# A streaming-encoder layer with 64 experts: expert outputs scattered with an add into two sums per token, in place of one row per token and choice

## The reference, cut to what matters

```python
def moe_ffn(h, ...):
    scores = sigmoid(t @ w_router)
    ...                                   # 4 of 8 groups, then top 8 of 64 experts: idx
    gate = sel / sum(sel) * 2.5
    yb = (silu(xb @ we_gate[e]) * (xb @ we_up[e])) @ we_down[e]     # for each block of tokens of an expert
    routed = segment_sum(yb * gate, tok)                            # 8 rows a token
    shared = (silu(t @ ws_gate) * (t @ ws_up)) @ ws_down
    return routed + shared

x = x + gt2 * rmsnorm(moe_ffn(h, ...), norm_ffn_post)
```

## Time and profile before

| what | value |
|---|---|
| median of 3 runs | 1409.8 us |
| the profiled execution | 1406.37 us |
| its span, first to last instruction | 1404.6 us |
| granted TensorE clock, mean | 0.965 of full speed |
| busy: TensorE, VectorE, ScalarE, GpSimd | 1297.7, 1010.8, 617.2, 256.0 us |
| experts, first instruction to the barrier | 618.7 to 1352.2 us |
| last stage | 1352.2 to 1404.6 us |
| moved by DMA | 340.8 MB, 243 GB/s over the span |

### The profile page before, as it was taken

How to read it: one execution, slowest core, us unless ns; L and a number is a source line. 1 busy time by engine, 2 the same in 40 slices (tenths; PEclk the granted TensorE clock), 3 DMA queues, 4 the chain that set the end, 5 groups by cost and what they waited for, 6 DMA issues and landing times. The chain is left out here.

```text
span 1404.6 us, 18781 instructions
## 1 busy us (share of the span) xinstructions
PE 1297.7 (92%) x5779; PEld 914.4 (65%) x5779; DVE 1010.8 (72%) x1651; ACT 617.2 (44%) x944; POOL 256.0 (18%) x329
## 2 busy tenths in 40 slices
PE   4999999858998999969999999999999999999947
PEld 4878888546884444536767677676776767776613
DVE  5879999789343523646878888788887888878617
ACT  3523222542242013134656566565665656656401
POOL 0000000250000000012233232332323323232200
PEclk9899999979998999989999999999999999999979
DMA  9773353100017321328999999999999999989268
GB/s 351 279 255 132 110 173 113 60 1 1 1 61 288 110 90 60 150 103 325 347 356 351 349 358 349 356 350 359 381 380 363 344 343 348 351 321 328 105 260 346
DMA packets 86890, 340.82 MB, mean 243 GB/s; under 512 B 17122, under 2 KB 22452, under 8 KB 59708
## 3 DMA queue, kind: packets, MB, share of 16 engines
q1 hardware_dynamic: 66960, 306.51, 58.3%
q0 software_dynamic: 19584, 33.60, 6.6%
q10 hardware_dynamic: 300, 0.11, 0.0%
HBM read 333.87 MB, written 44.04 MB: 269 GB/s over the span
## 5 line engine op out<-in xcount | busy, mean ns | idle before, releaser
L2261 DVE TENSOR_TENSOR gate_up_low<-gate_up,gate_up_high 128x1024 fp32r<-128x1024 f32 x204 | 244.6, 1220 | 42.5 <-ACT gate_up_high L2152 42.5
L2233 PE MATMUL py<-down_ring,hT 128*128 128x512 f32 x544 | 250.0, 602 | 1.0 <-ACT hT L2171 0.9
L2194 PE MATMUL p_gate_up<-gate_up_high,x_hi 128*128 128x512 f32 x544 | 242.4, 446 | 5.3 <-DVE x_lo L2270 5.3
L2194 PE MATMUL p_gate_up<-gate_up_low,x_hi 128*128 128x512 f32 x544 | 216.8, 398 | 0.0
L2194 PE MATMUL p_gate_up<-gate_up_high,x_lo 128*128 128x512 f32 x544 | 215.4, 396 | 0.0
L2152 ACT ACTIVATE gate_up_high<-gate_up 128x1024 fp32r<-128x1024 f32 x204 | 203.7, 1051 | 0.3 <-PEq L1415 0.3
L2233 PEld LDWEIGHTS py<-down_ring,hT 128*128 128x128 f32 x544 | 98.0, 190 | 99.0 <-issue 98.9
L2194 PEld LDWEIGHTS p_gate_up<-gate_up_high,x_hi 128*128 128x128 f32 x544 | 103.9, 191 | 44.6 <-issue 20.9
L2123 POOL TENSOR_TENSOR carrier<-offsets 1x1 f32<-1x1 f32 x136 | 30.7, 226 | 517.8 <-DVE tokens L2279 471.1
L2194 PEld LDWEIGHTS p_gate_up<-gate_up_high,x_lo 128*128 128x128 f32 x544 | 103.5, 190 | 30.1 <-issue 11.0
L2176 ACT ACTIVATE y<-py 128x512 f32<-128x512 f32 x68 | 40.7, 599 | 180.1 <-PE py L2233 180.1
(11 more groups left out here) (361 smaller groups left out, 1928.6 us busy)
## 6 DMA issues: line engine op xcount, KB each, us to landing
down_ring<-in_we_down SPq DMA_DIRECT2D x68, 1024.0 KB, 9.5
gate_up<-in_we_gate SPq DMA_DIRECT2D x51, 1024.0 KB
gate_up<-in_we_up SPq DMA_DIRECT2D x51, 1024.0 KB
x_again<-in_we_gate SPq DMA_DIRECT2D x17, 1024.0 KB
x_again<-in_we_up SPq DMA_DIRECT2D x17, 1024.0 KB
ring<-in_w_in SPq DMA_DIRECT2D x8, 2048.0 KB, 7.9
ring<-in_w_ada SPq DMA_DIRECT2D x16, 1024.0 KB, 5.9
rows<-expert_rows SPq DMA_DIRECT2D x6, 2048.0 KB, 18.5
```

The source lines that it names most:

```text
L2194: mm = pe.matmul(pgu[u % 2][:, :], x[:, u % 2, k, :], weights, start=(k == 0 and n == 0), stop=(k == KD - 1 and n == 2))
L2233: mm = pe.matmul(py[half][:, :], hT[:, u % 2, k, :], weights[:, k, half * N:half * N + N], start=(k == 0), stop=(k == 1))
L2261: V.tensor_tensor(moe.low[u % RING][:, :, piece(i), :], moe.gate_up[u % RING][:, :, piece(i), :], exact(w_hi[:, u % 2, :, piece(i), :]), A ...
```

## The change

A block's outputs are no longer scattered to rows of their own. There are two arrays in DRAM of one row a token; blocks of even number are scattered with an add to the first, those of odd number to the second. The first is preset with the shared expert's output, the second with zeros, both by SyncE at the start of `experts`; the zeros come from the two `y` buffers, which GpSimd clears first. A scatter waits for the scatter two blocks back, that is the one before it into the same array. The row number is the token number, so the rank and the third table value go. The last stage loads two rows a token, 4 MB in place of 16.8 MB, adds them on VectorE, and doesn't use TensorE.

```diff
             def tabulate():
-                for t in range(NT):
-                    link.sign(V.tensor_tensor_scan(rank[:, t, :], keep.ones[:, 0:NE], sel[:, t, :], 0.0, ALU.mult, ALU.add))
...
-                link.sign(V.tensor_tensor(rank, rank, sel, ALU.subtract))
...
-                for t in range(NT):
-                    link.sign(V.tensor_scalar(values[:, t, :, 2], rank[:, t, :], tokf[:, 2, t:t + 1], None, ALU.add))
...
-    moe.parts = m.sb("table_parts", [P, NT, NE, 3, 3], BF16)
+    moe.parts = m.sb("table_parts", [P, NT, NE, 2, 3], BF16)
...
-    moe.rows = nc.dram_tensor("expert_rows", (S * TOPK, D), F32, kind="Internal").ap()
+    moe.sums = [nc.dram_tensor(f"expert_sums{i}", (S, D), F32, kind="Internal").ap() for i in range(2)]
...
             sp.wait_ge(s_x, 1)
+            sp.dma_start(moe.sums[0].rearrange("(t p) d -> p t d", p=P), moe.shared[:, :, :]).then_inc(s_start, 16)
+            sp.wait_ge(s_zero, 1)
+            for half in range(2):
+                sp.dma_start(moe.sums[1][half * S // 2:(half + 1) * S // 2, :].rearrange("(t p) d -> p t d", p=P),
+                             y[:, :, :]).then_inc(s_blank, 16)
             for b in range(RING - 1):
                 moe.load_down(sp, b, b)
...
         def _(pool):
+            pool.memset(y[:, :, :], 0.0).then_inc(s_zero, 1)
...
                 pool.wait_ge(s_yV, b + 1)
+                if isinstance(b, int) and b < 2:
+                    pool.wait_ge(*((s_start, 16), (s_blank, 32))[b])
+                left(pool, b, u)
                 carry_wait(s_scatter, b, 1)
-                pool.indirect_dma_start(moe.rows, bass.IndirectOffsetOnAxis(row_ids[:, u % 4, 0:1], 0), y[:, u % 2, :], None,
-                                        bounds_check=last_row, oob_is_err=False).then_inc(s_out[u % 2], 16)
+                pool.indirect_dma_start(moe.sums[u % 2], bass.IndirectOffsetOnAxis(row_ids[:, u % 4, 0:1], 0), y[:, u % 2, :], None,
+                                        bounds_check=last_token, oob_is_err=False,
+                                        compute_op=ALU.add).then_inc(s_out[u % 2], 16)
...
             def y_half(b, u, first):          # on ScalarE and on VectorE
+                if isinstance(b, int) and b < 2:
+                    act.wait_ge(s_blank, 32)
...
-                    mm = pe.matmul(pid[:, 0:9], hot[:, u % 2, t, :], column[:, u % 2, t, :], start=(t == 0), stop=(t == NT - 1))
+                    mm = pe.matmul(pid[:, 0:6], hot[:, u % 2, t, :], column[:, u % 2, t, :], start=(t == 0), stop=(t == NT - 1))
...
-                V.tensor_tensor(row_ids[:, u % 4, :], number[:, u % 4, 2:3], moe.offsets[:, 1:2], ALU.add).then_inc(s_rows, 1)
+                V.tensor_tensor(row_ids[:, u % 4, :], number[:, u % 4, 1:2], moe.offsets[:, 0:1], ALU.add).then_inc(s_rows, 1)
```

The new last stage (the old one's loads, products, tree and halves go):

```diff
+            for t in range(NT):                                    # SyncE
+                for kind, tile in enumerate((y, more)):
+                    sp.dma_start(tile[:, t, :], moe.sums[kind][t * P:(t + 1) * P, :]).then_inc(s_in[t], 16)
...
+                act.activation(sq[:, :], y[:, t, :], ACT.Square, accum_out=total[:, t:t + 1]).then_inc(s_sq, 1)
+                act.wait_ge(s_sq, t + 1)
+                act.activation(mean[:, t:t + 1], total[:, t:t + 1], ACT.Copy, bias=D * RMS_EPS).then_inc(s_whole, 1)
...
+            def gated(t):                                          # VectorE
+                dve.wait_ge(s_in[t], 32)
+                V.tensor_tensor(y[:, t, :], y[:, t, :], more[:, t, :], ALU.add).then_inc(s_y, 1)
+                dve.wait_ge(s_y, t + 1)
+                V.scalar_tensor_tensor(out=scaled[:, t, :], in0=y[:, t, :], scalar=D ** 0.5, in1=keep.gate2[:, :],
+                                       op0=ALU.mult, op1=ALU.mult).then_inc(s_gt, 1)
...
+            gated(0)
+            for t in range(NT):
+                if t + 1 < NT:
+                    gated(t + 1)
+                finish(t)
```

More of the change, by code:

```diff
@@ L1407 @@
 MAXB = NE + S * TOPK // P - 1
-NO_TOKEN, NO_ROW = 8 * S, 16 * S * TOPK
+NO_TOKEN = 8 * S
 BIG = 1e30
@@ L1441, in merge_route @@
         g8 = old(NT, NG, 8)
-        scores, biased, sel, gated, left, rank = (old(NT, NE) for _ in range(6))
-        values = old(NT, NE, 3)
+        scores, biased, sel, gated, left = (old(NT, NE) for _ in range(5))
+        values = old(NT, NE, 2)
         gs, top4, top8 = (old(NT, 8) for _ in range(3))
         gleft, gmask = old(NT, NG), old(NT, NG)
-        total, over, tokf, pf, bf = old(NT), old(NT), old(3, NT), old(1), old(4)
+        total, over, tokf, pf, bf = old(NT), old(NT), old(2, NT), old(1), old(4)
         before = old(P)
@@ L1791, in _ @@
             link.sign(V.tensor_scalar(tokf[:, 1, :], tokf[:, 0, :], float(-NO_TOKEN), None, ALU.add))
-            link.sign(V.tensor_scalar(tokf[:, 2, :], tokf[:, 0, :], float(TOPK), float(-NO_ROW), ALU.mult, ALU.add))
             dve.wait_ge(s_x, 16)
@@ L1867, in tabulate @@
                     link.sign(V.tensor_scalar(values[:, t, :, 1], sel[:, t, :], 0.0, tokf[:, 1, t:t + 1], ALU.mult, ALU.add))
-                link.wait()
-                for t in range(NT):
-                    link.sign(V.tensor_scalar(values[:, t, :, 2], rank[:, t, :], tokf[:, 2, t:t + 1], None, ALU.add))
                 link.wait()
@@ L1952, in plan_experts @@
     moe.n_blocks = m.sb("n_blocks", [1, 1], I32)
-    moe.offsets = m.sb("offsets", [P, 2])
+    moe.offsets = m.sb("offsets", [P, 1])
     moe.xg = m.sb("xg", [P, 4, D])
@@ L1983, in experts @@
         hot = m.sb("hot", [P, 2, NT, P], BF16)
-        column = m.sb("column", [P, 2, NT, 9], BF16)
-        number = m.sb("number", [P, 4, 3])
+        column = m.sb("column", [P, 2, NT, 6], BF16)
+        number = m.sb("number", [P, 4, 2])
         tokens = m.sb("tokens", [P, 4, 1], U32)
@@ L2013, in experts @@
         s_out = [m.sem(f"p5_scattered{i}") for i in range(2)]
+        s_start, s_zero, s_blank = m.sem("p5_shared_stored"), m.sem("p5_zeros_made"), m.sem("p5_zeros_stored")
         block = stack.enter_context(nc.Block())
@@ L2116, in _ @@
         def _(pool):
-            last_token, last_row = pool.to_reg(S - 1), pool.to_reg(S * TOPK - 1)
+            last_token = pool.to_reg(S - 1)
+            pool.memset(y[:, :, :], 0.0).then_inc(s_zero, 1)
             def carry_wait(semaphore, b, place):
@@ L2276, in numbers @@
                 taken(dve, s_x, b, 4)
-                V.tensor_reduce(number[:, u % 4, :], pid[:, 0:9].rearrange("p (v j) -> p v j", j=3), AX.X, ALU.add).then_inc(s_sum, 1)
+                V.tensor_reduce(number[:, u % 4, :], pid[:, 0:6].rearrange("p (v j) -> p v j", j=3), AX.X, ALU.add).then_inc(s_sum, 1)
                 dve.wait_ge(s_sum, b + 1)
@@ L2298, in y_half @@
                 dve.wait_ge(s_y, b + 1)
+                if isinstance(b, int) and b < 2:
+                    dve.wait_ge(s_blank, 32)
                 left(dve, b, u)
@@ L2309, in combine @@
         m = Memory(nc, stack)
-        H = TOPK // 2
-        rows = m.sb("rows6", [P, NT, TOPK, D])
         x1 = moe.x1
[L2313 to L2324, removed]
+        y, scaled, more = (m.sb(name, [P, NT, D]) for name in ("y6", "scaled6", "odd6"))
+        sq = m.sb("sq6", [P, D])
+        total, mean, rstd = m.sb("total6", [P, NT]), m.sb("whole6", [P, NT]), m.sb("rstd6", [P, NT])
+        s_in = [m.sem(f"p6_sums{t}_in") for t in range(NT)]
+        s_y = m.sem("p6_sums_added")
+        s_gt, s_sq, s_whole, s_r = m.sem("p6_y_gated"), m.sem("p6_squared"), m.sem("p6_squares"), m.sem("p6_rstd")
         s_o, s_st = m.sem("p6_out"), m.sem("p6_stored")
-        s_a = m.sem("p6_scalar_chain")
         block = stack.enter_context(nc.Block())
-        expert_rows = moe.rows.rearrange("(t p j) d -> t p j d", p=P, j=TOPK)
-        LAST = NT - 1
         def cols(half):
@@ L2347, in _ @@
             sp.wait_ge(s_st, 16 * 2 * NT)
[L2349 to L2358, removed]
         @block.gpsimd
@@ L2363, in _ @@
                 pool.wait_ge(s_whole, t + 1)
-                pool.tensor_tensor(rstd[:, t:t + 1], whole[:, t:t + 1], keep.power[:, 0:1], ALU.pow).then_inc(s_r, 1)
+                pool.tensor_tensor(rstd[:, t:t + 1], mean[:, t:t + 1], keep.power[:, 0:1], ALU.pow).then_inc(s_r, 1)
         @block.scalar
         def _(act):
-            link = Link(act, s_a)
             for t in range(NT):
-                act.wait_ge(s_y, 2 * t + 1)
+                act.wait_ge(s_y, t + 1)
                 if t:
[L2372 to L2378, removed]
+                    act.wait_ge(s_sq, t)
+                act.activation(sq[:, :], y[:, t, :], ACT.Square, accum_out=total[:, t:t + 1]).then_inc(s_sq, 1)
+                act.wait_ge(s_sq, t + 1)
+                act.activation(mean[:, t:t + 1], total[:, t:t + 1], ACT.Copy, bias=D * RMS_EPS).then_inc(s_whole, 1)
         @block.vector
@@ L2382, in _ @@
             V = nc.vector
[L2383 to L2404, removed]
+            def gated(t):
[3 more added lines that the diff above has]
```

(23 more changed lines are left out.)

1 line of the change is left out of this document (removed).

## The result

The changed kernel takes 1430.6 us (median of 4 runs, 1428.85 to 1433.86) against 1409.72 beside it: ratio 1.016, 95% interval 1.0147 to 1.0172. It is slower by 21 us where 26 us less were forecast, and outside the range. The profiled execution has a span of 1432.0 us against 1404.6, 27.4 more; it is the slowest of the changed kernel's four (1433.86), and that of before (1406.37) was a quick one, so some 6 us of the 27.4 are chance between executions.

The account below looks back on a forecast made before the run. The loop was taken as bound by TensorE, with DMA close behind at 0.93, and the last stage by its loads. Terms -29.1 + 0.3 + 0 + 2.5 = -26.3 took 1409.8 to 1383.5 us, range 1378 to 1406.

Parts of the forecast that it names:

- Loop: 0: Expert loop: the adding scatter doubles to 1.40 us, giving 10.34 us a block, TensorE's pace, so no time change.
- The second view: Loop window 1019.60:1040.20: 399 GB/s, 4.11 MB a block without TensorE gaps, against 3.87 MB needed by the mean block.
- Rival D: Loop: a memory-side ceiling of 363 GB/s makes a block 10.66 us; +8, 1392; chance 0.04.
- Rival B: Loop, 660 to 1300: becomes DMA-bound, an add costing three times a scatter; +31.5, 1415; chance 0.12.
- the ring: Loop's weight loads: issued far enough ahead that 12.5 us of lateness can pile up before TensorE waits.
- Rival A: Loop: an add costs the engines two and a half times a scatter; +10, 1394 (1389 to 1406); chance 0.14.
- The last stage: Final stage: loads stop being the end, VectorE's 15.8 us of work sets it; -29.1 us (-27 to -31).
- The end of the experts: Last eight blocks: GpSimd waits for each scatter, adds land 2 us later; +2.5 us (0 to 8).
- Rival C: Last eight blocks: an add lands 5 us later, over four waits; +13, 1397; chance 0.07.
- The start: Start of the experts: GpSimd's clearing of y, 1.76 us, delays its first carrier and gather; +0.3 us (0 to 2).
- The presets: Start of the experts: SyncE's 4.2 MB of stores ahead of down loads; worth 0, at most 10 without cover.

Follow-up runs that it names:

- e1: Changed kernel with each block's tokens dealt over all 128 partitions in steps of four instead of filling from 0 upwards; 1380.66 us, ratio 0.9799 to before.
- e6: Changed kernel with a block's first 64 tokens placed in every other group of four neighbouring partitions; 1435.83 us (one execution).
- e7: Changed kernel with a block's first 64 tokens in the even partitions, the rest in the odd ones; 1380.24 us (one execution).
- e8: Changed kernel where only even-numbered blocks scatter with an add and odd-numbered ones write without adding; 1393.86 us (one execution).
- e2: Changed kernel with a scatter that writes without adding, with presets, waits and reading back kept; 1379.27 us (one execution).
- e9_best: e5 with GpSimd clearing y after its second gather instead of before the first; 1375.03 us, ratio 0.9774 to the kernel before.
- e5: e1 with SyncE's load of x1 waiting for the last block's gate and up products instead of its down product; 1376.70 us, ratio 0.9775 to before.

## Why the prediction was wrong

**The step that failed** is in the loop: "All queues together take 93.3 us of 100, 9.64 of 10.33 us a block, so 0.69 us are free", and from it "9.64 + 0.70 = 10.34, just the pace of TensorE". The 0.70 for the add was right (0.75 in e1, 0.66 in the changed kernel). The 9.64 was a mean over 16 engines, taken for the load of each. A load of weights is complete when its last part is: in the changed kernel twelve of sixteen have landed after 8.7 us and the last after 27.9. So the fullest engines count, if a part is an engine's. By the estimate from bytes they had 9.9 us of work in 10.3, and the add brought them not 0.7 but 1.2 (twice the 0.75 of e1 would be 1.5). In place of "Loop: 0" the loop cost 44.8 us, 11.15 us a block. e6 and e7 show the cause: the same rows and bytes, 1435.8 against 1380.2 us.

**The second view was misread as well.** The 399 GB/s of 1019.60:1040.20 came with TensorE at full pace, so I took 4.11 MB a block to be possible. The queues of that window show what was in it:

```profile
q1 hardware_dynamic: 891, 6.49, 79.6%
q0 software_dynamic: 561, 1.73, 20.8%
```

1.73 MB for two gathers and two scatters are 0.43 each, 106 rows of 4 KB where a mean block has 60. So these were well-filled blocks, which use most of the partitions: a rather even window, and I priced the lopsided ones by it. Rival D was rejected with the same window; D is not what happened, but the reason given was weak.

**Rival B** had the place and the direction, but too small a size (44 us of excess in the loop, less 12.5 that the ring holds, so 31.5 and 1415; measured 44.8 net, 1430.6) and not the mechanism: it asked for three times a scatter, and got a chance of 0.12. That the ring holds a debt shows in the ten blocks at the old pace before the first gap. Ten blocks at 0.87 over the pace are 8.7 us, and 27 at 0.25 in e8 are 6.8: by this estimate it holds 7 to 9 us and not 12.5, with the presets' share not taken apart.

**Rival A's figures** don't follow from its sum: a factor of 2.3 gives 1385 and one of 2.9 gives 1411, not 1389 and 1406. The top of the range rests on them. At 2.9 it would have been 5 us higher, still far below 1430.6.

**The last stage** was right by its own steps: VectorE's 15.8 us of work, begun 5 us after the first issue; -29.3 against -29.1. With an even deal the forecast holds, as one sum: e1 gives 1380.7 for 1383.5 forecast, with the loop at TensorE's pace and the DMA share at 0.99 as said, and the stretch behind the last y at +3.1 for +2.5. That is no excuse, since the kernel on record isn't e1.

**The end of the experts** cost +8.8 against +2.5 (0 to 8). The timeline of POOL in the changed kernel shows where: the scatter of block 66 leaves at 1386.54, beside the 2 MB load of x1 issued at 1386.84, and the last one waits for it:

```profile
1386.54 1.56 POOL L2142 DMA_INDIRECT expert_sums<-y,row_ids  x1 [0.46 <-issue]
1397.53 0.18 POOL L2123 TENSOR_TENSOR carrier<-offsets 1x1 f32<-1x1 f32 x1 [9.43 <-DMA expert_sums<-y,row_ids]
1398.17 1.56 POOL L2142 DMA_INDIRECT expert_sums<-y,row_ids  x1 [0.46 <-issue]
```

I had added up delays of each scatter, but not asked what runs beside the last two. In e2, without the add, GpSimd didn't wait there and the stretch was 13.2 us; in e1, 16.3, where my +2.5 meets +3.1; the rest of the 8.8 goes with the lopsided order (not taken apart further). Rival C (four waits in the last eight blocks) shows as five waits of POOL, 43.5 us in place of 22.4 in three, but I find no loss of TensorE's in them: its one long block there, 13.2 us, follows a wait of 3.18 us of ScalarE for weights.

**The start** cost 1.1 us for the clearing in place of 0.3; the reason is the last section's. The other 1.1 of the stretch's +2.2 is not taken apart; e1 doesn't have it (35.7 us to the first y, against 36.7). The presets cost no wait, as forecast: stores issued from 629.70, the slowest landed 13.1 us after its issue, y first written at 656.3.

## What to carry to other kernels

The DMA share of these views is a mean over 16 engines. Before adding traffic to a loop that is close to it, ask which partitions the rows of a partly filled transfer sit in, and price the fullest engines: here, by the estimate from bytes, some 60 rows in partitions 0 to 63 counted about double, and one reordered table was worth 50 us (1430.6 to 1380.7). Look at when each part of a transfer lands, and not only the last. When a window seems to prove room, work out what was in it before pricing others by it. The add in a scatter cost the engines about as much again as the write (0.75 us in e1, beside 0.70 for the plain scatter of before); that alone was hidden in e1.

## What the runs showed of the hardware that I had not expected

A clearing on GpSimd stopped a copy on VectorE. Timelines of the changed kernel at the start of the experts, then of e9_best, where the clearing comes later:

```profile
619.62 1.85 DVE L2298 COPY column<-table_parts 128x24 bf16<-128x24 bf16 x1 [10.00 <-PEq L1415]
...
619.64 1.80 POOL L2117 MEMSET y<- 128x2048 f32 x1 [53.85 <-POOLq L1415]
...
622.28 0.64 POOL L2123 TENSOR_TENSOR carrier<-offsets 1x1 f32<-1x1 f32 x1 [0.83 <-DVE tokens L2285]
```

```profile
618.87 0.17 DVE L2299 COPY column<-table_parts 128x24 bf16<-128x24 bf16 x1 [10.00 <-PEq L1415]
...
620.42 0.64 POOL L2122 TENSOR_TENSOR carrier<-offsets 1x1 f32<-1x1 f32 x1 [55.38 <-DVE tokens L2286]
```

The copy of 24 bfloat16 a partition takes 1.85 us beside the clearing of 1.80, and 0.17 without it (1.85 beside 1.80 or 1.81 too in e1, e2, e5, e6, e7 and e8, which all clear first); so the first gather's token numbers are late too, 2.68 us from the stage's first instruction to the carrier against 1.57. I had priced only GpSimd's own queue. The copy ended with the clearing (at 621.47, the clearing at 621.44); the rows don't show what held it.

GpSimd's scatter instruction is also slightly dearer with the add: at the end of the stage 1.56 us against 0.99 in e2_plain. It is hidden, since GpSimd is busy under 40 us of 100 in the loop (38.13 in e1).
